# Retention products in a two-layer hybrid backbone: heads alternate between the halves of the array, state products first, 64-column state updates

## The reference

```
def _chunk_states(kc, vc, log_decay, init):
    zeta, chunk_decay = _state_decay(log_decay)
    u = jnp.einsum('bnjhd,hj,bnjhe->nbhde', kc, zeta, vc)

    def step(state, u_n):
        return chunk_decay[None, :, None, None] * state + u_n, state

    final, prev = lax.scan(step, init, u)
    return prev, final

def retention_scan(q, k, v, log_decay, init):
    ...
    scores = jnp.einsum('bnihd,bnjhd->bnhij', qc, kc) * intra
    o_intra = jnp.einsum('bnhij,bnjhe->bnihe', scores, vc)
    prev, final = _chunk_states(kc, vc, log_decay, init)
    o_cross = jnp.einsum('bnihd,hi,nbhde->bnihe', qc, xi, prev)
    return (o_intra + o_cross).reshape(B, T, H, d), final
```

## Time and profile before

| what | value |
|---|---|
| median of three runs | 1689.31 us (1688.16 to 1696.31) |
| the profiled execution: its span | 1692.4 us |
| PE busy | 1618.0 us (96%) |
| DVE, POOL, ACT busy | 953.3, 806.6, 326.4 us |
| chain of work that ended last, by engine | PE 52%, DVE 16%, issue 13%, POOL 8%, DMA 7% |

### The profile page before, as it was taken

The page is one execution under the profiler, slowest core; times in us unless marked ns, Lnnn a source line. Parts: engine busy times, 40 slices in busy tenths (PEclk is TensorE's granted clock), DMA queues, the critical chain, the costliest instruction groups (busy, mean ns, idle before and its releaser), DMA issues.

```text
span 1692.4 us, 23806 instructions
## 1 busy us (share of the span) xinstructions
PE 1618.0 (96%) x8620; PEld 1344.0 (79%) x8620; DVE 953.3 (56%) x1310; ACT 326.4 (19%) x489; POOL 806.6 (48%) x636
## 2 busy tenths in 40 slices
PE   8989999989899999999999999999989999999997
PEld 2778788778778888888888888877767787887876
DVE  2797554277787875884288648454456441341445
ACT  2502111230312200220022214111221220120220
POOL 1144232275344454444444444452465666676664
PEclk9899999999899999999999999999999999999998
DMA  8244111233133243331333222221122222222222
GB/s 345 95 153 165 45 38 38 68 135 131 62 124 125 100 154 124 118 136 64 110 124 112 90 97 77 87 86 50 63 75 87 85 89 98 91 95 99 99 87 99
DMA packets 49633, 174.42 MB, mean 103 GB/s; under 512 B 6448, under 2 KB 6832, under 8 KB 48560
## 3 DMA queue, kind: packets, MB, share of 16 engines
q1 hardware_dynamic: 45504, 167.79, 28.1%
q10 hardware_dynamic: 4080, 5.94, 1.3%
HBM read 167.41 MB, written 2.10 MB: 100 GB/s over the span
## 4 chain that ended last, share of the span: by engine, by line
PE 52%; DVE 16%; issue 13%; POOL 8%; DMA 7%; ACT 2%; DVEq 1%; ACTq 0%; POOLq 0%; SPq 0%
PE pair L1005 43%; DMA raw<-in_slabs 6%; POOL w_lo L384 5%; DVE aux L616 3%; POOL w_hi L382 2%; PE pair L1054 2%; DVE tg L947 2%; DVE tv L947 2%; PE aux L1210 1%; DVE hid_lo L975 1%; PE aux L1181 1%; PE aux L1196 1%; DVE modv L619 1%; PE aux L1215 1%; DVE tv L972 1%
## 5 line engine op out<-in xcount | busy, mean ns | idle before, releaser
L1005 PE MATMUL pair<-h_hi,w_hi 128*128 128x512 f32 x1888 | 572.0, 361 | 20.2 <-POOL w_lo L384 12.3
L1005 PE MATMUL pair<-h_lo,w_hi 128*128 128x512 f32 x1888 | 563.9, 356 | 7.2 <-DVE h_lo L721 5.5
L1005 PE MATMUL pair<-h_hi,w_lo 128*128 128x512 f32 x1888 | 563.8, 356 | 0.0
L384 POOL TENSOR_TENSOR w_lo<-raw,w_hi 128x1024 fp32r<-128x1024 f32 x210 | 535.1, 2548 | 17.5
L380 POOL TENSOR_TENSOR gate<-ones 128x1 f32<-128x1 f32 x210 | 56.3, 268 | 848.4 <-PE pair L1005 753.7
L1005 PEld LDWEIGHTS pair<-h_hi,w_hi 128*128 128x128 f32 x1888 | 311.4, 191 | 75.8 <-issue 18.2
L1005 PEld LDWEIGHTS pair<-h_lo,w_hi 128*128 128x128 f32 x1888 | 311.4, 190 | 66.7 <-DVE h_lo L721 13.3
L1005 PEld LDWEIGHTS pair<-h_hi,w_lo 128*128 128x128 f32 x1888 | 312.3, 191 | 49.6
L616 DVE CUSTOM_DVE_ANT_0 aux<-mod_slot,c_b 128x1024 f32<-128x1024 f32 x160 | 231.3, 1445 | 5.6 <-DMA mod_slot<-in_mods 2.8
L382 POOL TENSOR_SCALAR w_hi<-raw 128x1024 fp32r<-128x1024 f32 x210 | 223.4, 1064 | 0.1
L1005 PE MATMUL pair<-hid_hi,w_hi 128*128 128x512 f32 (+1 forms) x528 | 160.6, 358 | 5.6 <-POOL w_lo L384 4.9
(11 more groups left out here) (137 smaller groups left out, 1129.7 us busy)
## 6 DMA issues: line engine op xcount, KB each, us to landing
raw<-in_slabs SPq DMA_DIRECT2D x210, 512.0 KB, 3.2
mod_slot<-in_mods SPq DMA_DIRECT2D x80, 512.0 KB, 3.2
start_slot<-in_start_mods SPq DMA_DIRECT2D x8, 1024.0 KB, 13.8
x<-in_x SPq DMA_DIRECT2D x4, 768.0 KB, 18.2
rot<-kT ACTq DMA_DIRECT2D x32, 64.0 KB, 2.0
rot<-Y ACTq DMA_DIRECT2D x32, 64.0 KB, 2.0
out<-fin SPq DMA_DIRECT2D x8, 256.0 KB, 2.2
c_b<-in_c SPq DMA_DIRECT2D x1, 512.0 KB, 4.2
```

What stands on the lines that cost most here:

```text
L384: nc.gpsimd.tensor_tensor(w_lo[p][:, :], raw[p][:, :], w_hi[p][:, :].bitcast(fp32), ALU.subtract).then_inc(split, 1)
L1005: ins = nc.tensor.matmul(out[:, a:b], wt, xt[:, a:b], start=first and k == 0, stop=last and k == 2)
```

## The change

Three edits, all in TensorE's program:

1. The state update makes, instead of one 128x128 product for each block, one 64x64 product for each head, at the same place of the same bank: weights of 64 columns, 64 moving columns, output on the head's 64 partitions. That is 16 products in place of 8, in two halves of the array's columns that alternate.
2. In "scores" the loops over heads and blocks change places: the two halves of the array's rows alternate from block to block, where before one half did its four blocks and then the other.
3. In "out" all state products come first, for all blocks, and the value products follow. The first product of the step alone clears the bank.

```
                         for b in range(HB):
-                            ins = nc.tensor.matmul(aux(3)[:, b * P:b * P + P], ktok[:, c, b * P:b * P + P],
-                                                   vz[:, 2 * b:2 * b + 2, :], start=True, stop=True)
+                            for hh in range(2):
+                                lo = b * P + HD * hh
+                                ins = nc.tensor.matmul(aux(3)[HD * hh:HD * hh + HD, lo:lo + HD],
+                                                       ktok[:, c, lo:lo + HD], vz[:, 2 * b + hh, :],
+                                                       start=True, stop=True)
...
-                        for hh in range(2):
-                            r = slice(HD * hh, HD * hh + HD)
-                            for b in range(HB):
+                        for b in range(HB):
+                            for hh in range(2):
+                                r = slice(HD * hh, HD * hh + HD)
                                 ins = nc.tensor.matmul(aux(hh)[:, b * CH:b * CH + CH], kT[r, b, col:col + CH],
                                                        Y[r, b, col:col + CH], start=True, stop=True)
...
+                        begun = False
+                        for d, st in ((0, fwd), (1, bwd)):
+                            if st is None:
+                                continue
+                            for b in range(HB):
+                                nc.tensor.matmul(aux(2)[:, b * CH:b * CH + CH], state[st[0]][:, st[1], b, :],
+                                                 qxi[:, d, b, :], start=not begun, stop=True, skip_group_check=begun)
+                                begun = True
                         for b in range(HB):
-                            out = aux(2)[:, b * CH:b * CH + CH]
-                            begun = False
-                            for d, st in ((0, fwd), (1, bwd)):
-                                if st is not None:
-                                    nc.tensor.matmul(out, state[st[0]][:, st[1], b, :], qxi[:, d, b, :],
-                                                     start=not begun, stop=True, skip_group_check=begun)
-                                    begun = True
                             for hh in range(2):
```

## The result

The changed kernel took 1673.86 us in the median of 4 runs (1672.94 to 1678.89); the kernel before, run beside it, 1689.09 (1688.16 to 1696.31). The ratio is 0.9905, with an interval of 0.9886 to 0.9925. The forecast was 1670.4 us, 3.5 us less, and the range holds the measured time. Three later measurements of the same program, each beside its own runs of the kernel before, gave 1673.77, 1670.28 and 1670.97 us, with ratios of 0.9897, 0.9881 and 0.9891. Over its own runs of the kernel before, the four gained 15.2, 17.4, 21.4 and 17.9 us, where 18.9 was forecast; the forecast as a ratio, 0.9888, lies inside the interval of each. The profiled execution of the first measurement is the slowest of its four, with a span of 1677.0 us.

What follows compares the result with a forecast made beforehand. TensorE was taken as the bound, with a TensorE-DVE-TensorE chain at some layer 1 states. "Out" -10.5, scores -4.9 and states -3.5 sum to -18.9 us, from 1689.3 to 1670.4 us; range 1664 to 1680.

Steps and rivals of the forecast that it cites:

- Out: Ten "out" steps: fewer changes of shape save 1.04 us with one state, 1.05 with two; -10.5 us.
- Scores: Ten scores steps: alternating row halves start together, 1.54 us instead of 2.09; -4.9 us, ends 0 and -6.0.
- States: Twenty state updates: 0.11 us less at 13 that did not wait, 0.28 at 7 that waited; -3.5 us.
- Pace of 128 columns: Rival at state updates: 64-column products keep 0.11 us a pair, states +5.2 us, 1679.1 us in all; chance 0.14.
- Scores do not overlap earlier: Rival in scores: the lower half still joins late in any order; -14.0 us, 1675.3 us; chance 0.08.
- DVE as the bound: Rival in layer 1: "out" and scores of four chunks lose savings to DVE waits; -13.1 us, 1676.2 us; chance 0.09.
- Column halves one at a time: Rival at state updates: 16 products go singly, 1.17 us more a state; +6.8 us, 1696.1 us; chance 0.03.
- The clock: Rival at layer 1's first scores: half clock avoided or caused, 3 us either way; clear gain beyond the forecast, chance 0.06.

Runs made afterwards that it cites:

- e12: The changed kernel with no edit, measured a fourth time against the kernel before: 1670.97 us, ratio 0.9891.
- e5: Changed kernel, but "out" in two groups of two blocks, state products then value products in each: 1675.8 us.
- e6: Changed kernel, but in the scores the row halves alternate every two blocks instead of every one: 1676.97 us.
- e3: Kernel before with only the first edit, the 64-column state updates: 1686.86 us, ratio 0.9966.
- e8: Changed kernel, but each 64-column product of the state update moves all 128 columns of its block's values: 1676.48 us.
- e7: Changed kernel, but in the state update one column half does its four blocks, then the other: 1674.49 us.

## Why the prediction was right, and where it was off

**The bound and the method held.** A step priced from the pair of tiles ahead to the second pair behind came out in the changed trace to within 0.03 us of its forecast for "out" (2.82 and 3.71 against 2.80 and 3.69), for the scores (1.55 against 1.54) and for states (1.51 against 1.48). What TensorE saved in the retention stretches was 10.8 + 9.8 = 20.6 us in the first trace of the change. Of this 1.6 us is clock, 6.8 us at half clock in layer 1 having become 3.4. At like clock it is 19.0 us, and 18.9 to 19.1 in the other three traces. The sum was 18.9. That they agree to a tenth is in part luck: the terms measured alone come to 17.9.

**Where the first measurement lost its 4 us.** The span of its profiled execution fell by 15.4 us only, because 317.27 to 1108.83 us, where the change touches nothing, took 791.6 us instead of 784.1. The same stretch before:

```profile
331.49:1115.62 784.13, 760.86 (x4274) 660.03 (x4274) 531.51 (x739) 151.64 (x213) 373.26 (x285) 0.98 0.32 110
```

Of the 7.4 us more, PE is busy for 5.3, with the same 4274 products; it stood at half clock for 37.5 us of the stretch, where it was 27.3 before (30.7 to 34.1 in the three later traces). The other 2.1 us are idle time. Among its waits one grew, in layer 0's MLP, and others shrank. PE's wait there (340 to 530 us) in the first trace of the change:

```profile
PE pair L1005 <- DVE tv L947: 7.8, 3, 3.6
```

Before, it was one wait of 3.5 us. DVE was late after dot products that ran beside weight splits on POOL. Timeline of DVE and of POOL, first trace of the change:

```profile
487.87 3.24 DVE L616 CUSTOM_DVE_ANT_0 aux<-mod_slot,c_b 128x1024 f32<-128x1024 f32 x1
...
486.78 3.24 POOL L384 TENSOR_TENSOR w_lo<-raw,w_hi 128x1024 fp32r<-128x1024 f32 x1
```

The same in e12, the fourth trace of the same program:

```profile
487.36 1.22 DVE L616 CUSTOM_DVE_ANT_0 aux<-mod_slot,c_b 128x1024 f32<-128x1024 f32 x1
...
484.92 2.40 POOL L384 TENSOR_TENSOR w_lo<-raw,w_hi 128x1024 fp32r<-128x1024 f32 x1
```

Where the two overlap, both records are longer: 3.24 us instead of 1.22 on DVE, and 3.24 instead of 2.40 on POOL. The Trainium skill, "SBUF — State Buffer", Who interferes with whom, says that DVE and GpSimd share a port pair that one instruction holds to its end, also where a DVE operation with two inputs in SBUF meets a GpSimd one that reads SBUF. The rows fit that: DVE's record ends 1.09 us after POOL's, near the 1.22 that it takes alone, and POOL's began while an earlier dot product ran on DVE (486.12 to 487.78 us). Such meetings are in every trace (the longest dot product takes 3.40 us before the change and in e12); here PE waited behind them. I first held that the change brings this about, by the time at which the MLP starts. That theory fell. In the three later traces PE waits for `tv` once (3.5 to 3.9 us), and the stretch between the retentions takes 783.6, 784.2 and 782.1 us, as before the change. Everything outside retention takes 1421.6 us before, and 1426.7, 1423.8, 1418.8 and 1417.9 in the four traces of the change. It varies by 9 us, with the clock's dips among it, and no trend. What sets the time of such a meeting in one execution was not tried and stays open. The first trace is of the slowest of its four runs, so it does not account for their median. The 3.5 us between forecast and first median cannot be told from the spread between executions: the forecast lies between the last two medians (1670.28 and 1670.97) and 3.4 us below the first two.

**Term by term.** *"Out"*, -1.04 and -1.05 us a step: right (1.02 and 1.03 measured), and e5 shows its cause, 0.35 us for each turn of shape. *Scores*: 0.54 for 0.55. That the lower half joins late because eight products stand ahead of it in the order was the open end of that term (0 was its other bound); e6 shows it. The first scores of layer 1 were counted with 1.0 us, as if they ran at half clock again. In the first trace of the change they began at full clock and were busy 1.27 us instead of 3.09; the clock fell 0.9 us after their start, and in e12 not at all. Most of that gain is clock, which the comparison at like clock takes out. For the last two chunks of layer 1 the gain was put at nothing, since `qxi` had taken 4.20 us in the third. Timeline of POOL before, beside that `qxi`, then of DVE in that chunk of the change:

```profile
1193.15 2.67 POOL L384 TENSOR_TENSOR w_lo<-raw,w_hi 128x1024 fp32r<-128x1024 f32 x1
...
1179.26 2.14 DVE L839 TENSOR_TENSOR qxi<-Y,xi 128x512 f32<-128x512 f32 x2
```

DVE took 2.14 us for the same two operations, and "out" did not wait there, so the third chunk did gain. This is the reading that the term had wrong: 4.20 us was taken as what `qxi` costs there, but it ran beside a weight split on POOL (1192.01 to 1195.82 us with line 382). In the fourth chunk before, where none was under way, it took 1.29. *States*: the pace of a pair is 0.058 us where 0.055 was taken, so 0.08 us was saved for 0.11 at a state that did not wait, and 0.25 for 0.28 at one that did: 13 x 0.08 + 7 x 0.25 is 2.8 us, 0.7 less than the term by these blocks; the stretches of e3 give 3.5, and where the 0.7 comes from stays open. The term's own parts, 1.4 and 2.0, add up to 3.4 and not 3.5.

**The rivals.** *Pace of 128 columns*: false, and e8 shows what it would have been, 0.42 us more a state. *Scores do not overlap earlier*: false, 8 of 16 have begun after 0.55 us. *DVE as the bound*: false, PE's waits for `vz` and `Y` in layer 1 grew by 0.5 us in all, and that for `St` went. *Column halves one at a time*: false; 16 products begin in 0.46 us, where one at a time, 15 x 0.11, it would be 1.65. The rule of the Trainium skill that was set against this term ("TensorE: Matmul & The Clock Gate", Part 3, The mechanism) speaks of weight loads alone; read as the prediction reads it, it would have given that, and the trace disagrees for these column halves too, with the same 0.46 us. *The clock*: it did move, by 1.5 to 1.6 us for each dip in the retention stretches, and in both directions from one execution to the next. Against the trace before, it is 1.6 us of the gain in these stretches in the first trace of the change and 4.7 in e12, so the bound of 3 us was too narrow.

## What to carry to other kernels

Count how often a small step changes the shape of its products: here a turn between whole and half columns and back cost 0.35 us, and sorting the products of ten steps by shape saved 10 us with no instruction less. Alternate halves of the array product by product, since behind eight products of one half the other joined only at about the fifth. Price a step from the tile ahead of it to the second tile behind, and check the sum in the stretch where the change acts, at like clock, before looking for a gain or a loss in the whole time.

## What the runs showed that was not expected

- DVE's reciprocal of 128x512 takes 3.35 us, where that of 128x8 takes 0.20: 6.2 ns for each further column. A copy of 128x512 takes 0.43 us. I had priced it like a copy.
- A DVE operation that takes 1.22 us alone took 3.24 us beside one on POOL; 9 us of spread between executions of the same program lie outside the code that was changed.
- The second half of the array joined at about the fifth product of the first whichever way it was split: row halves in the scores before (4 begun after 0.55 us) and column halves in e7 (0.75 us from first start to last instead of 0.46).
